# Both gate matrices of a head as one 64-row, 128-column weight in a hybrid mixer and MoE layer

## The reference

```python
xc = causal_depthwise_conv(rg_x, rg_conv_w) + rg_conv_b
xh = xc.reshape(bsz, s, RG_HEADS, RG_HEAD_DIM)
r = sigmoid(einsum("bshi,hij->bshj", xh, gate_a_w).reshape(bsz, s, D_RG) + gate_a_b)
i = sigmoid(einsum("bshi,hij->bshj", xh, gate_x_w).reshape(bsz, s, D_RG) + gate_x_b)
log_a = -RG_C * r * softplus(-lam)
a = exp(log_a)
u = sqrt(-expm1(2.0 * log_a)) * (i * xc)
h = associative_scan(a * h + u)
y_rg = h * gelu(rg_gate)
y_sc = sc_b * causal_depthwise_conv(sc_c * sc_v, sc_conv_w)
mix = concatenate([y_rg, y_sc]) @ w_out
```

## Time and profile before

| | |
|---|---|
| time, median of 3 runs | 457.89 us (457.72 to 459.35) |
| the profiled execution | 457.27 us, its span 455.5 us |
| PE busy | 415.1 us (91%), 2588 products |
| ACT busy | 107.5 us (24%) |
| DVE busy | 187.6 us (41%) |
| projection and output projection | about 10 to 174 us, the first layer norm and the router to about 192 us |
| experts | about 193 to 424 us; the last part is the sum and the second layer norm |

### The profile page before, as it was taken

One profiled execution on the slowest core, in us unless ns is written; L12 is line 12 of the kernel. 1 busy time (PEld: TensorE's weight loads), 2 busy tenths in 40 slices (PEclk: granted clock), 3 DMA queues, 4 the chain that ended last, 5 costly groups with the idle time before them and its releaser, 6 DMA issues.

```text
span 455.5 us, 6659 instructions
## 1 busy us (share of the span) xinstructions
PE 415.1 (91%) x2588; PEld 281.8 (62%) x2588; DVE 187.6 (41%) x372; ACT 107.5 (24%) x175; POOL 84.9 (19%) x116
## 2 busy tenths in 40 slices
PE   7999999999999999889999999997967988868882
PEld 6888766888888888655555655555544645444330
DVE  2579222999745485763212222212112112120085
ACT  3442457751140014101111111111101111111311
POOL 2500000000000003162233332233113101011033
PEclk9999999999999999999999999999989989999997
DMA  8956222022379999399999999999999999998383
GB/s 293 276 192 202 94 92 90 4 94 92 109 279 391 413 416 383 138 370 358 408 407 408 411 406 408 413 409 411 411 411 410 409 415 413 415 416 331 142 337 139
DMA packets 44479, 139.09 MB, mean 305 GB/s; under 512 B 5287, under 2 KB 15559, under 8 KB 40358
## 3 DMA queue, kind: packets, MB, share of 16 engines
q1 hardware_dynamic: 38288, 126.89, 71.8%
q0 software_dynamic: 6144, 11.84, 7.3%
q10 hardware_dynamic: 22, 0.02, 0.0%
HBM read 134.41 MB, written 12.58 MB: 323 GB/s over the span
## 4 chain that ended last, share of the span: by engine, by line
PE 71%; DMA 19%; SPq 3%; DVE 3%; issue 1%; ACT 1%; DVEq 0%; POOLq 0%
PE bank L1047 18%; DMA wgu<-in_exp_w_up 16%; PE bank L878 11%; PE bank L879 11%; PE bank L880 11%; PE bank L1066 8%; PE bank L1125 2%; PE bank L1037 2%; PE bank L1057 2%; PE bank L930 2%; SPq L494 2%; DMA raw<-in_w_in 1%; DMA pair_y<-y_pairs 1%; SPq L491 1%; PE bank L977 1%
## 5 line engine op out<-in xcount | busy, mean ns | idle before, releaser
L1047 PE MATMUL bank<-wgu,xTg 128*64 128x256 f32 x992 | 120.3, 397 | 19.9 <-DMA wgu<-in_exp_w_up 18.8
L1047 PEld LDWEIGHTS bank<-wgu,xTg 128*64 128x64 f32 x992 | 74.9, 143 | 56.4 <-issue 17.9
L1425 DVE TENSOR_TENSOR hid<-gated,bank 64x256 f32<-64x256 f32 x32 | 13.5, 422 | 125.6 <-ACT gated L811 125.6
L878 PE MATMUL bank<-xT_hi,w_hi 128*128 128x512 f32 x160 | 62.8, 393 | 1.8 <-DVE w_lo L1158 1.8
L652 POOL DMA_INDIRECT y_pairs<-ys,y_rows x32 | 32.3, 1011 | 161.0 <-PE bank L1037 106.0
L879 PE MATMUL bank<-xT_lo,w_hi 128*128 128x512 f32 x160 | 62.3, 390 | 0.0
L880 PE MATMUL bank<-xT_hi,w_lo 128*128 128x512 f32 x160 | 62.3, 389 | 0.0
L1066 PE MATMUL bank<-wdn,hidT 128*64 128x512 f32 x248 | 58.7, 593 | 0.9 <-issue 0.9
L811 ACT ACTIVATE gated<-bank 64x256 f32<-64x256 f32 x32 | 12.1, 379 | 158.6 <-PE bank L1047 158.6
L1144 DVE TENSOR_TENSOR w_lo<-raw,w_hi 128x2048 fp32r<-128x2048 f32 x12 | 27.5, 2291 | 33.0 <-ACT w_hi L726 32.9
L726 ACT ACTIVATE w_hi<-raw 128x2048 fp32r<-128x2048 f32 x12 | 23.0, 1920 | 59.9 <-PE bank L880 53.2
(11 more groups left out here) (237 smaller groups left out, 429.3 us busy)
## 6 DMA issues: line engine op xcount, KB each, us to landing
wgu<-in_exp_w_gate SPq DMA_DIRECT2D x31, 1024.0 KB, 15.3
wgu<-in_exp_w_up SPq DMA_DIRECT2D x31, 1024.0 KB, 21.5
wdn<-in_exp_w_down SPq DMA_DIRECT2D x31, 1024.0 KB, 20.6
raw<-in_w_in SPq DMA_DIRECT2D x9, 1024.0 KB, 5.3
raw<-in_w_out SPq DMA_DIRECT2D x4, 1024.0 KB, 5.0
pair_y<-y_pairs SPq DMA_DIRECT2D x8, 512.0 KB, 7.4
xres<-in_x SPq DMA_DIRECT2D x2, 1024.0 KB, 6.8
h_rows<-xres POOLq DMA_DIRECT2D x4, 512.0 KB, 8.0
```

Source lines behind the costliest of these rows:

```text
L878: pe.matmul(dst, a_hi, b_hi, start=start, stop=False)
L1047: mm = pe.matmul(psum[2 + b][BLOCK * which:BLOCK * which + BLOCK, 0:F], xTg[b][:, j, h * BLOCK:(h + 1) * BLOCK], wgu[s][:, which, k, :], s ...
```

## The change

A head's two gate matrices stand side by side in one tile `wg` of 64 rows (a head) and 128 columns (a, then x). A channel tile then needs two products in place of four: head 0 in the upper 64 rows of the array, head 1 in the lower 64, each over all 128 columns and each into a bank of its own. Bank q now holds head q: gate a in partitions 0 to 63, gate x in 64 to 127. The sigmoids have to put this back in channel order, so each of the two per tile becomes two of 64 partitions; for half of them the source is in the other half of the partitions than the destination. Since the bias is read beside the source, a second small tile `bias_across` holds the parameters with the halves of each channel tile exchanged. It is made by eight products behind the four turns after chunk 0, and by one more DVE copy.

```diff
-        wga = at("wga", [P, CT, 64], F32, shared_y + 4096)
-        wgx = at("wgx", [P, CT, 64], F32, shared_y + 6144)
+        wg = at("wg", [P, CT, 2, 64], F32, shared_y + 4096)
+        bias_across = at("bias_across", [P, CT, PARAMS], F32, shared_y + 6144)
...
-            for w, dst in ((rg_gate_a_w, wga), (rg_gate_x_w, wgx)):
-                pool.dma_start(dst[:, :, :], w.rearrange("(a b) i j -> (b i) a j", b=2)).then_inc(gates_in, 16)
+            for which, w in enumerate((rg_gate_a_w, rg_gate_x_w)):
+                pool.dma_start(wg[:, :, which, :], w.rearrange("(a b) i j -> (b i) a j", b=2)).then_inc(gates_in, 16)
...
-            act.wait_ge(par_ready, 1)
+            act.wait_ge(par_ready, 2)
...
-                        act.activation(gr[j][:, :], psum[4 + 2 * (j % 2)][:, :], ACT.Sigmoid, bias=par[:, j, P_AB:P_AB + 1]).then_inc(gates_ready, 1)
-                        act.activation(gi[j][:, :], psum[5 + 2 * (j % 2)][:, :], ACT.Sigmoid, bias=par[:, j, P_XB:P_XB + 1]).then_inc(gates_ready, 1)
+                        for which, dst, at_bias in ((0, gr[j], P_AB), (1, gi[j], P_XB)):
+                            src = slice(64 * which, 64 * which + 64)
+                            for q in range(2):
+                                bias = (par if q == which else bias_across)[src, j, at_bias:at_bias + 1]
+                                act.activation(dst[64 * q:64 * q + 64, :], psum[4 + 2 * (j % 2) + q][src, :], ACT.Sigmoid, bias=bias).then_inc(gates_ready, 1)
...
-                        act.wait_ge(gates_ready, 2 * j + 1)
+                        act.wait_ge(gates_ready, 4 * j + 2)
...
+                    for j in range(CT):
+                        for q in range(2):
+                            other = j * P + 64 * (1 - q)
+                            mm = pe.matmul(psum[7][64 * q:64 * q + 64, (CT + j) * PARAMS:(CT + j + 1) * PARAMS],
+                                           par_rows[:, other:other + 64], ident[0:PARAMS, 0:PARAMS], start=True, stop=True)
                     mm.then_inc(par_turned, 1)
...
-                            pe.wait_ge(gates_ready, 2 * (j - 2) + 2)
-                        for w, bank in ((wga, psum[4 + 2 * (j % 2)]), (wgx, psum[5 + 2 * (j % 2)])):
-                            for q in range(2):
-                                h = slice(64 * q, 64 * q + 64)
-                                mm = pe.matmul(bank[h, :], w[h, j, :], conv[j][h, :], start=True, stop=True)
+                            pe.wait_ge(gates_ready, 4 * (j - 2) + 4)
+                        for q in range(2):
+                            h = slice(64 * q, 64 * q + 64)
+                            mm = pe.matmul(psum[4 + 2 * (j % 2) + q][:, :], wg[h, j, :, :].rearrange("p a n -> p (a n)"), conv[j][h, :], start=True, stop=True)
                         mm.then_inc(gates_summed, 1)
...
+            v.tensor_copy(bias_across[:, :, :], psum[7][:, CT * PARAMS:2 * CT * PARAMS].rearrange("p (j n) -> p j n", j=CT)).then_inc(par_ready, 1)
```

More of the change, by code:

```diff
@@ L917, in _ @@
                     for j in range(CT):
-                        mm = pe.transpose(psum[7][:, j * PARAMS:(j + 1) * PARAMS], par_rows[:, j * P:(j + 1) * P], ident[0:PARAMS, 0:PARAMS])
+                        pe.transpose(psum[7][:, j * PARAMS:(j + 1) * PARAMS], par_rows[:, j * P:(j + 1) * P], ident[0:PARAMS, 0:PARAMS])
+                    for j in range(CT):
[3 more added lines that the diff above has]
+                                           par_rows[:, other:other + 64], ident[0:PARAMS, 0:PARAMS], start=True, stop=True)
                     mm.then_inc(par_turned, 1)
```

## The result

| | before | after |
|---|---|---|
| time, median of 12 runs each, same chip | 459.07 us (457.72 to 460.86) | 460.99 us (459.76 to 462.97) |
| ratio | | 1.0047, 95% interval 1.0032 to 1.0063 |
| the profiled execution, its span | 457.27 us, 455.5 us | 459.99 us, 458.1 us |
| PE busy / ACT busy | 415.1 us / 107.5 us | 413.8 us / 113.9 us |

The account below looks back on a forecast made before the run. PE, 71% of the chain of waits, was taken to bound the kernel. Of 2.85 us net gain on PE, 0.74 was left after the wait at chunk 8: 457.15 us against 457.89, range 455.4 to 459.2.

Parts of the forecast that it names:

- The gate products: On PE, row halves run together at 0.43 us a step: 1.72 us gained a batch, 3.44 in all.
- Rival 1: At the gates on PE, row halves with 128 columns don't run together: +0.98 us, 458.9; chance 0.12.
- The small products: On PE behind the four turns after chunk 0, eight products for the crossed bias add 0.59 us.
- The sigmoids: On ACT, eight half-width sigmoids a batch at 0.57 us each take 4.56; bounds for a crossing one 0.29 and 1.14.
- rival 3: On ACT, a sigmoid that crosses halves costs double: +1.54 us, 459.4, or +3.8, 461.7; chance 0.06.
- The absorption on DVE: DVE's 0.50 us idle time behind `drive` goes, so its lateness shrinks from 1.15 to 0.57 us.
- The wait at chunk 8: PE stands still about 2.1 us before chunk 8, released by DVE's `sc_pad`, and starts it at 106.77.
- The clock behind the wait: At PE's new wait ahead of chunk 8, full speed was assumed behind it, as behind an earlier idle of 1.80 us.
- The sum: Added up in time order to chunk 8 starting 0.74 us earlier, carried to the end: 457.15 us against 457.89.
- rival 4: At chunk 8, PE's clock falls in the new wait: +0.8 us, 458.7; chance 0.04.
- a gain of the mixer arrives at the end whole: From mixer to experts: the transfer-bound part hangs on PE too, so the mixer's gain or loss reaches the end whole.

Follow-up runs that it names:

- e4: The kernel before with each sigmoid split into two of 64 partitions that read and write the same half: 460.72 us, 1.0035.
- e9: The kernel after with the sigmoids of a batch reordered so that every second one has its predecessor's partitions: 458.31 us, 1.0044 to before.
- e6: The kernel after, unchanged, profiled once more: 458.17 us.
- e5: The kernel before, unchanged, profiled once more: 455.68 us.
- e11: The kernel after, unchanged, timed again on the chip of the third set: 460.65 us, 1.0087 to before.
- n14: The kernel after, unchanged, timed again on another chip in the fourth set: 460.74 us, 1.0079 to before.
- the filled ones: Two runs of the kernel after with 24 useless PE products in the wait ahead of chunk 8: 458.57 us, 1.0048, and 459.50 us, 1.0036 to before.
- the third set: Runs on one chip of the kernel after with paired sigmoids, with the wait filled and unchanged, and of before with DVE's reorder; before took 456.12 us.
- the fourth: Repeats on another chip of before, after, the filled wait and the reorder alone: 456.27, 460.74, 459.50 and 457.87 us.
- e1: The kernel after with the wide sigmoids of the kernel before, gates not put back in channel order: 456.09 us against 459.10, 0.9943.
- e2: The kernel after with the new gate form for the first batch only and the crossed bias from two DVE copies: 458.39 us, 0.9982 to before.
- The two controls of the reorder alone: Two runs of the kernel before with only DVE taking the first two banks of chunk 6 earlier: 458.26 us, 1.0038, and 457.87 us, 1.0019.
- e8: The kernel of e7 with the crossed bias from two DVE copies in place of the eight small products: 452.78 us, 0.9904 to before.
- e7: The kernel after with DVE taking the first two banks of chunk 6 ahead of the rounding of chunk 9: 453.95 us against 457.60, 0.9919.
- e3: The kernel before plus the eight small products and the second DVE copy, their result unused: 459.33 us, 1.0016.

## Why the prediction was wrong

- **The gate products** were right: 1.92 us a batch against a forecast of 1.86, a gain of 1.66 each. Rival 1 (row halves don't run together) is out.
- **The small products** were right: 0.57 us against 0.59.
- **The sigmoids are the step of the mixer's sum that failed.** "Halving the partitions saves next to nothing" holds; "I take 0.57" as the price of a half-width sigmoid does not. 0.57 was the distance of two neighbours that overlap, and overlap was taken over from a row in which all have the same 128 partitions. The price is 0.71, eight take 5.66 us in place of 4.56, and the first tanh comes 2.16 late in place of 1.15. The bounds, 0.29 and 1.14, held it; rival 3's reason (crossing) was wrong, as e4 and e9 show.
- **The absorption on DVE** was right: of 2.13 us lateness 1.55 is left (forecast: 0.58 of it absorbed).
- **The wait at chunk 8** was foretold in place and releaser, not in size: 3.16 us against 2.1. With 0.71 in the prediction's own sum chunk 8 would have moved by -0.74 + 8 x 0.14 = +0.38; measured +0.27 (after), +0.41 (e6 against e5). That alone would have made about 458.3, inside the range; so this step turns the gain into a small loss, and doesn't make up the whole of it.
- **The clock behind the wait is the second step that failed.** The sum priced the new wait by its length alone and left the clock to rival 4, at 0.04. At the wait of 3.2 us the clock fell in three of the four profiles of the kernel after (e6, e11, n14; not in the first), at a price of 1.5 to 1.6 us each, and in neither of the filled ones. The evidence used against it was one wait of 1.80 us with no fall, and it had little weight: it was a shorter wait at another place, and at that place two of eighteen profiles do show a fall.
- **The sum.** In the result the rows give 0.3 of the 1.9 us, and lost clock perhaps 1.3, against a before of other runs and with an interval as wide as itself. In the third set after stands 4.5 us above before, of which 0.3 to 0.4 are the late start of chunk 8 and 3.3 lost clock; in the fourth 3.5 us, 0.4 and 2.9. It is more lost clock than the one fall at chunk 8 can hold: e11 and n14 have a second stretch of 0.93 at 190 to 215 us, e6 has not. So lost clock is the larger part of the loss in these two sets, and the fall at chunk 8 a part of it.
- **Still open.** Why the whole of the excess goes when only the wait is filled is not shown; an idle PE there may shift what follows into other falls, but no run tests it. Nor is it shown why e1 and e2 lose 1.0 and 1.3 us more clock than before with no wait at chunk 8. The filled kernels stand 2.4 and 2.2 us above before in their medians, of which the rows give 0.4 and 0.5 and the clock 0.5 and 0.1: about 1.6 us in each have no row. The two controls of the reorder alone (+2.1, +0.6 us) have none either, while before against itself gave a ratio of 0.9998, so a difference of under about 2 us in one set is not explained here. Open too is the late start of DVE at the first expert in the first profile of after (1.17 us): it stands in e1 to e4 as well, and not in e6.

What e1 and e8 settle is that the gain of the gates is whole at chunk 8 as soon as nothing makes PE stand still there: 3.0 and 3.65 us earlier, and 3.0 and 4.8 at the end. That a gain of the mixer arrives at the end whole, as the prediction had it, is not general: of e2's 2.0 us 0.7 arrived.

## What to carry to other kernels

Take the price of an instruction from the distance of starts only if the new instructions stand to each other as the old ones did; if they change partitions, take the full duration, and look for an order in which neighbours share them. When a sum ends with the busiest engine standing still at a new place, price the clock behind that wait too, and look first at which operation the wait hangs on: here moving two DVE operations ahead of the rounding of a later chunk (e7) made of a kernel that lost 0.5 to 0.9% one that gains 0.8%. Before believing half a per cent, time the kernel against itself, and sum the granted clock over all runs rather than read it off one profile.

## What the runs showed of the hardware

- Two neighbours on ACT of 512 columns overlap by about 0.1 us when they read and write the same partitions (starts 0.57 to 0.59 apart, durations 0.67 to 0.70), and not at all when the half changes (0.69 to 0.71), whether or not source and destination halves differ. The Trainium skill, Advanced Engine Details and Errata, "The Read-Write Bubble", says that on ScalarE and VectorE the memory bus is pipelined within an instruction but not between two. The second case agrees; the first does better than that.
- Two float32 products in the row halves of the array, with 128 columns of weight each, run fully together: 8 passes with a change of shape in 1.92 us.
- At idle times of PE of 3.16 to 3.18 us ahead of chunk 8 TensorE's clock fell from 2.4 to 1.2 GHz in three executions of four; behind one of 2.64 us (e9) and one of 1.18 us (e4) at the same place it did not. Ahead of the first product of chunk 0, where the idle time is 1.32 to 2.35 us, it fell in two of eighteen, behind 2.16 us (e7) and 1.90 us (n14), and not behind 2.35 us (e3). So the length of the idle time alone doesn't decide in these runs. A fall at chunk 8 cost 1.5 to 1.6 us of PE time, and with 24 useless products in the gap there was none in either profile.
